# Twenty modulation tiles summed on VectorE during the projection stage of a two-layer trunk

## The reference

```python
mod = jnp.einsum('bd,lde->lbe', jax.nn.silu(c), mod_w) + mod_b[:, None, :]
for l in range(DEPTH):
    sh_m, sc_m, gt_m, sh_f, sc_f, gt_f = jnp.split(mod[l], 6, axis=-1)
    h = modulate(rms_norm(x, norm_w[l, 0]), sh_m, sc_m)
    y = hgrn2_ssd_mixer(...)  # layer 0: HGRN2 and SSD heads;  layer 1: rwkv7_mixer(...)
    x = x + gt_m[:, None, :] * y
    h = modulate(rms_norm(x, norm_w[l, 1]), sh_f, sc_f)
    x = x + gt_f[:, None, :] * grouped_moe(...)
```

## Time and profile before

| | us |
|---|---|
| time, median of 3 runs | 1276.27 (1276.25 to 1276.28) |
| the profiled execution's own time | 1273.94 |
| its span in the trace | 1272.2 |
| PE busy | 1162.0 (91%) |
| DVE busy | 398.7 (31%) |
| ACT busy | 268.5 (21%) |
| POOL busy | 84.7 (7%) |
| HBM read | 307.55 MB, 243 GB/s over the span |

### The profile page before, as it was taken

One profiled execution on the slowest core, in us unless ns is written; L12 is line 12 of the kernel. 1 busy time (PEld: TensorE's weight loads), 2 busy tenths in 40 slices (PEclk: granted clock), 3 DMA queues, 4 the chain that ended last, 5 costly groups with the idle time before them and its releaser, 6 DMA issues.

```text
span 1272.2 us, 15796 instructions
## 1 busy us (share of the span) xinstructions
PE 1162.0 (91%) x6545; PEld 742.2 (58%) x6546; DVE 398.7 (31%) x951; ACT 268.5 (21%) x443; POOL 84.7 (7%) x100
## 2 busy tenths in 40 slices
PE   4899999998898799999989699979988799989896
PEld 2775688873486544455444378648875544544353
DVE  0141322374611411111111584964432411111113
ACT  2212110414311211111101353233232111111113
POOL 5002121200000000000000001511000000000000
PEclk9899999999899799999999899989989899999898
DMA  9898462359884078929999830000378088999990
GB/s 353 274 387 318 166 223 108 132 194 381 350 294 169 1 259 308 394 108 394 394 394 367 285 133 1 1 1 2 132 268 328 1 319 305 395 394 394 394 372 33
DMA packets 139247, 309.35 MB, mean 243 GB/s; under 512 B 8032, under 2 KB 9404, under 8 KB 139196
## 3 DMA queue, kind: packets, MB, share of 16 engines
q1 hardware_dynamic: 138400, 307.39, 65.5%
q10 hardware_dynamic: 796, 1.23, 0.3%
HBM read 307.55 MB, written 1.05 MB: 243 GB/s over the span
## 4 chain that ended last, share of the span: by engine, by line
PE 66%; DMA 16%; DVE 8%; issue 4%; ACT 2%; SPq 2%; POOL 1%; ACTq 0%; DVEq 0%; POOLq 0%
DMA ring<-in_moe_w 14%; PE bank L1091 14%; PE bank L763 13%; PE bank L816 7%; PE bank L1115 4%; PE bank L1062 3%; PE bank L1055 3%; PE bank L796 3%; PE bank L774 2%; SPq L610 2%; DVE scratch L2347 1%; PE bank L879 1%; PE bank L1164 1%; DMA ring<-in_mod_w 1%; DVE arena L1896 1%
## 5 line engine op out<-in xcount | busy, mean ns | idle before, releaser
L1091 PE MATMUL bank<-ring,arena 128*64 128x512 f32 x992 | 230.8, 607 | 15.7 <-DMA ring<-in_moe_w 15.7
L763 PE MATMUL bank<-arena,ring 128*128 128x256 f32 x960 | 213.5, 384 | 2.7 <-ACT arena L1517 2.7
L763 PEld LDWEIGHTS bank<-arena,ring 128*128 128x128 f32 x960 | 183.6, 192 | 30.5 <-issue 5.3
L1091 PEld LDWEIGHTS bank<-ring,arena 128*64 128x64 f32 x992 | 76.0, 140 | 157.6 <-issue 147.6
L1115 PE MATMUL bank<-ring,arena 128*64 128x512 f32 x544 | 120.5, 595 | 0.0
L2221 DVE TENSOR_TENSOR arena<-arena,bank 128x512 f32<-128x512 f32 x17 | 11.7, 688 | 251.3 <-PE bank L1091 251.3
L816 PE MATMUL bank<-arena,ring 128*128 128x256 f32 x384 | 86.1, 388 | 2.9 <-issue 2.9
L816 PEld LDWEIGHTS bank<-arena,ring 128*128 128x128 f32 x384 | 74.8, 195 | 13.9 <-issue 3.2
L1062 PE MATMUL bank<-arena 128*128 128x256 f32 x336 | 79.0, 380 | 1.7 <-issue 1.7
L1115 PEld LDWEIGHTS bank<-ring,arena 128*64 128x64 f32 x544 | 37.6, 137 | 73.6 <-issue 73.6
L1055 PEld LDWEIGHTS bank<-arena 128*128 128x128 f32 x608 | 70.6, 195 | 13.8 <-issue 13.8
(11 more groups left out here) (362 smaller groups left out, 1269.9 us busy)
## 6 DMA issues: line engine op xcount, KB each, us to landing
ring<-in_moe_w SPq DMA_DIRECT2D x90, 2048.0 KB, 16.8
ring<-in_mod_w SPq DMA_DIRECT2D x24, 2048.0 KB, 11.8
ring<-in_ev_w_in SPq DMA_DIRECT2D x13, 2048.0 KB, 12.2
arena<-in_moe_w SPq DMA_DIRECT2D x6, 2048.0 KB, 16.8
ring<-in_od_w_rkv SPq DMA_DIRECT2D x6, 2048.0 KB, 12.3
ring<-in_ev_w_out SPq DMA_DIRECT2D x4, 2048.0 KB, 17.8
ring<-in_od_w_o SPq DMA_DIRECT2D x2, 2048.0 KB, 10.3
arena<-in_x ACTq DMA_DIRECT2D x1, 1024.0 KB, 9.0
```

The source lines that it names most:

```text
L763: mm = pe.matmul(ps[:, c * S:(c + 1) * S], w_cols(slot)[:, k, (2 * half + c) * P:(2 * half + c + 1) * P], src[:, k, :], start=(k == 0), st ...
L1091: mm = pe.matmul(bank[4 + half][e * C:(e + 1) * C, :], hgT[:, kb, e * C:(e + 1) * C], w_cols(slots[2 * half + e])[:, kb, :], start=(kb == ...
```

## The change

The modulation tiles 4 to 23 are no longer multiplied on PE. For each, `mod_sum(m)` on DVE forms the weighted sum of its eight blocks of 128 rows: one `tensor_scalar` and seven `scalar_tensor_tensor` over 128x512, each waiting for the one before. That leaves 128 partial sums for each column in one of four accumulators (`mod_acc`, in arena buffer 10). PE adds these over the partitions in `mod_direct(m)`: four matmuls with the accumulator as weights and one column of ones. The accumulators alternate, so `mod_sum(m)` waits until `mod_direct(m - 4)` is done (semaphore `mod_full`), and `mod_direct(m)` waits for `mod_summed`.

The tiles of layer 1 come into the projection stage: one modulation tile behind each of in-tiles 0 to 3, and two behind each of in-tiles 4 to 11. PE's `modulation_step` in the HGRN steps and heads is gone. DVE takes the results of both layers in one place, between the last score copies and the convolution. ACT waits for the last `mod_direct` before it writes `gT`, which lies in the same buffer as the accumulators. The four sums of weights 0 to 3 stay on PE.

```diff
     for n, j in enumerate((2, 3, 0, 1, 4, 5, 12, 10, 11, 8, 9, 6, 7)):
         first.append(("in", 0, j))
-        if MOD_FIRST + n < 12:
-            first.append(("mod", 0, MOD_FIRST + n))
-    first += [("mod", 1, j) for j in range(12)]
+        for _ in range(1 if n < 4 else 2):
+            if m < MOD_DVE:
+                first.append(("mod", m // 12, m % 12))
+                m += 1
...
+                if kind == "mod" and MOD_FIRST <= 12 * l_mod + j < MOD_DVE:
+                    sp.wait_ge(mod_summed, 12 * l_mod + j + 1 - MOD_FIRST)
...
+            def mod_direct(m):
+                pe.wait_ge(mod_summed, m - MOD_FIRST + 1)
+                for q in range(4):
+                    mm = pe.matmul(bank[6][:, 4 * m + q:4 * m + q + 1], mod_acc[m % 4][:, q * P:(q + 1) * P],
+                                   ones[:, 0:1], start=True, stop=True)
+                mm.then_inc(mod_full, 1)
...
-                if MOD_FIRST + n < 12:
-                    modulation(MOD_FIRST + n, bank[7])
-                elif MOD_FIRST + n == 12:
-                    mod_columns(1, bank[6])
+                for m in {4: (4, 5, 6), 5: (7, 8, 9), **{n: (2 * n - 2, 2 * n - 1) for n in range(6, 13)}}.get(n, ()):
+                    mod_direct(m)
...
+            act.wait_ge(mod_full, MOD_DVE)
             evac_T(gT, 0, ACT.Silu)
...
+            def mod_sum(m):
+                slot, count = mod_slot(m)
+                acc = mod_acc[m % 4]
+                dve.wait_ge(tile_landed[slot], 16 * count)
+                dve.wait_ge(mod_full, max(MOD_FIRST, m - 3))
+                link(ts_(acc, w_cols(slot)[:, 0, :], csilu[:, 0:1], None, ALU.mult))
+                for k in range(1, KB):
+                    ins = stt(acc, w_cols(slot)[:, k, :], csilu[:, k:k + 1], acc, ALU.mult, ALU.add)
+                    if k < KB - 1:
+                        link(ins)
+                ins.then_inc(mod_summed, 1)
...
+            mod_sum(MOD_FIRST)
             dve.wait_ge(proj_evac, 4)
...
             level_diff(0)
             level_diff(1)
+            for m in range(5, 10):
+                mod_sum(m)
...
             for i in range(8):
                 level_mult(i)
+                for m in range(10 + 2 * i, min(12 + 2 * i, MOD_DVE)):
+                    mod_sum(m)
                 if i < 7:
                     level_take(i)
...
-            dve.wait_ge(mod_cols, 2)
-            modulation(0, 4 * MOD_FIRST, 48, bank[6]).then_inc(mod_taken, 1)
+            dve.wait_ge(mod_full, MOD_DVE)
+            mod_take(0, 4 * MOD_FIRST, 48)
+            mod_take(1, 0, 48).then_inc(mod_taken, 1)
             dve.wait_ge(mod_taken, 2)
             gains(0, 1)
+            gains(1, 0)
+            gains(1, 1)
```

More of the change, by code:

```diff
@@ L59 @@
 MOD_FIRST = 4
+MOD_DVE = 24
 NSUB = 4
@@ L86, in weight_tiles @@
     first = [("mod", 0, j) for j in range(MOD_FIRST)]
+    m = MOD_FIRST
     for n, j in enumerate((2, 3, 0, 1, 4, 5, 12, 10, 11, 8, 9, 6, 7)):
         first.append(("in", 0, j))
-        if MOD_FIRST + n < 12:
-            first.append(("mod", 0, MOD_FIRST + n))
-    first += [("mod", 1, j) for j in range(12)]
+        for _ in range(1 if n < 4 else 2):
+            if m < MOD_DVE:
+                first.append(("mod", m // 12, m % 12))
+                m += 1
     first += [("out", 0, j) for j in range(4)]
@@ L237, in trunk @@
         mod_full = sem("mod_full")
+        mod_summed = sem("mod_summed")
         mod_row = sem("mod_row")
@@ L281, in trunk @@
         dtz = sem("dtz")
-        dtabs = sem("dtabs")
         dtln = sem("dtln")
@@ L339, in trunk, with mod_slot @@
         M = [dict(shared, **{n: sem(f"m{l}_{n}") for n in moe_names}) for l in range(LAYERS)]
-        mod_rows = [buf(10)[:, 0:W], buf(10)[:, W:2 * W], buf(1)[:, 0:W]]
-        slide = [buf(i)[:, 2 * W:2 * W + KB * 63].rearrange("p (k n) -> p k n", k=KB) for i in (10, 10, 1)]
-        MOD_GROUPS = ((0, MOD_FIRST), (MOD_FIRST, 12), (12, 24))
+        mod_rows = [buf(10)[:, 0:W]]
+        slide = [buf(10)[:, 2 * W:2 * W + KB * 63].rearrange("p (k n) -> p k n", k=KB)]
+        MOD_GROUPS = ((0, MOD_FIRST),)
         def mod_group(m):
             return [g for g, (a, b) in enumerate(MOD_GROUPS) if a <= m < b][0]
+        mod_acc = [buf(10)[:, i * W:(i + 1) * W] for i in (0, 1, 3, 2)]
+        def mod_slot(m):
+            return plan[0][places[0, "mod"][m]][1:]
         qT, kT, bT, zT, gT = blocks(2), blocks(4), blocks(5), blocks(11), blocks(10)
@@ L507, in wait_used @@
                 at = places[l, kind].index(n)
-                if kind == "mod":
+                if kind == "mod" and MOD_FIRST <= 12 * l_mod + j < MOD_DVE:
+                    sp.wait_ge(mod_summed, 12 * l_mod + j + 1 - MOD_FIRST)
+                elif kind == "mod":
                     sp.wait_ge(mod_full, 12 * l_mod + j + 1)
@@ L799, in modulation @@
                 mm.then_inc(mod_full, 1)
-            mod_next = [12]
-            def modulation_step():
-                if mod_next[0] < 24:
-                    if mod_next[0] == 12:
-                        pe.wait_ge(basics, 3)
-                    modulation(mod_next[0], bank[0])
-                    mod_next[0] += 1
+            def mod_direct(m):
[4 more added lines that the diff above has]
+                mm.then_inc(mod_full, 1)
             def out_projection(stage, first, n, srcs, ready):
@@ L929, in _ @@
                 mm.then_inc(o_full, 1)
-                modulation_step()
             pe.wait_ge(dt_ready, 1)
@@ L1006, in _ @@
             mm.then_inc(stat_full, 1)
-            pe.wait_ge(mod_taken, 3)
             out_projection(0, places[0, "out"][0], 4, lambda i: oa[:, i, :] if i < KB else yT[:, i - KB, :],
@@ L1595, in _ @@
             evac_xbc(0)
-            mod_evac(1, bank[7])
             level_exp(4)
@@ L1601, in _ @@
             act.wait_ge(dtz, 1)
-            act.activation(dts[:, 1, :], dts[:, 0, :], ACT.Abs).then_inc(dtabs, 1)
-            act.wait_ge(dtabs, 1)
+            link(act.activation(dts[:, 1, :], dts[:, 0, :], ACT.Abs))
             act.wait_ge(small_landed, 16 * 7)
@@ L1871, in modulation, with mod_take @@
                            by_chunk(cols("mod_b", 48 * l + a, 48 * l + b)), ALU.add)
+            def mod_sum(m):
[9 more added lines that the diff above has]
+                ins.then_inc(mod_summed, 1)
+            def mod_take(l, a, b):
+                c = 48 * l + a
+                return tt_(modT[:, l, a:b], bank[6][:, c:c + b - a], cols("mod_b", c, c + b - a), ALU.add)
             def gains(l, f):
@@ L2070, in _ @@
                     ssd_out((h - 4) // 2)
-            dve.wait_ge(mod_cols, 3)
-            modulation(1, 0, 48, bank[2]).then_inc(mod_taken, 1)
-            dve.wait_ge(mod_taken, 3)
-            gains(1, 0)
-            gains(1, 1)
             dve.wait_ge(stat_rstd, 5)
```

7 lines of the change are left out of this document (removed).

## The result

The changed kernel takes 1346.29 us (1345.57 to 1346.58, 4 runs) against 1276.26 us for the kernel before on the same chip (1275.72 to 1276.28, 4 runs), a ratio of 1.0517 (95% interval 1.0477 to 1.0558). The forecast was 1318 us, with a range of 1302 to 1330: slower was right, the size was not. The mean granted clock went from 0.957 to 0.907.

What follows compares the result with a forecast made beforehand. The prediction took PE to set the time, with other engines level at levels 0 and 6. Terms +5.4 +12.8 +5.1 +8.2 +4.3 +12.7 +2.5 -9.9 gave +41, so 1318 us on the median, range 1302 to 1330.

Steps and rivals of the forecast that it cites:

- the four waits: PE waits at levels 0 and 1 for DVE, level 6 for POOL's product, and the convolution for ACT's SiLU; 76%.
- The price of a sum: On DVE, one tile's `tensor_scalar` and seven `scalar_tensor_tensor` take 6.0 us, bounds 5.4 and 6.6.
- steps 1, 4 and 6: Added delay up to level 0, +5.4 us; from level 5 to level 6, +8.2; from level 7 to SiLU, +12.7.
- the term from SiLU to head 0: Between the convolution's SiLU and the SSD heads, PE restarts after a long idle spell: +2.5 us.
- rivals A and B: A: DVE has room, nothing waits, 1261 us, 3%. B: levels on time, only the convolution late, 1284 us, 7%.
- C: Rival: DVE becomes the bound at every level, with sums nearer 7.5 us or POOL's steps slower: 1335 us, 10%.
- D: Rival: transfers come late as SP waits for DVE ahead of each in-tile, some 5 us at two or three levels: 1330, 4%.
- Step 7: In the SSD heads, eight modulation steps at 1.53 us go, less two `ssd_out` of 0.9 that come later: -9.9 us.
- So I let it shift as a block: Everything behind the SSD heads (output projection, experts, layer 1) keeps its order and ring slots: no added time.
- Step 3: Levels 2 to 5: PE stays the bound, narrowly, with 2.6 us more modulation work and a 2.5 us restart: +5.1.
- Steps 2 and 5: Level 0 to level 1: DVE's late sum and a 2.5 us restart, +12.8. Level 6 to level 7: `mod_direct` and restart, +4.3.
- a changed length of these stages: Sign of being wrong: the stages behind the output projection change their length.

Runs made afterwards that it cites:

- first experiment: The changed kernel with 16 extra 128x512 matmuls, used by nobody, while PE waits for the convolution's SiLU: 1347.1 us, ratio 1.0495.

## Why the prediction was right and wrong

The direction, the four waits and their releasers were right, and the experiments on order bear them out one by one: 12.9 of the 20.6 us at level 1, all of the wait at level 6 and all 12.6 us at the convolution went by moving instructions that do the same work. The price of a sum (6.0 us), steps 1, 4 and 6 and the term from SiLU to head 0 hold within 0.6 us. Steps 4 and 6 hold term by term; at step 1 there was luck. VectorE was free for the takes 0.9 us sooner than forecast (125.1 for 126.0), and from there to level 0 it took 6.3 us for the 4.9 "as before", as the second half of the diagonal ran at a lower clock (3.52 us; all of it took 4.00 in before). The rivals A and B needed levels on time, and didn't come. C wanted TensorE to idle for VectorE at levels 2 to 5, but it was busy for 96.00 of 96.00 us there. D had transfers late: neither TensorE nor VectorE waited for one between level 0 and the convolution.

The forecast's terms add up to +41.1 us (its last line has 41.3, a slip of 0.2), the measure is +71.6. Of the 30.5 missing:

- **Step 7, the heads: 13.2 us.** "Eight at 1.53" took the pitch of heads 8 to 15 as a property of a head. It was one of a head at full clock. In the changed kernel the clock fell ahead of the third decay row, and from there on a head took 2.62. Where the clock was brought back (the block in head 3), the stretch took 53.2 us. From the forecast's own terms, 58.5 of before + 2.5 - 9.9, and 3.5 for the block, it would be 54.6: the mechanism was right, its clock was not. Removing the wide matmuls from the loop removed what had kept the clock up, or brought it back.
- **The last part: 7.4 us.** "So I let it shift as a block" was wrong by 0 to 10 us for any kernel of this set, as its clock differs from kernel to kernel. The prediction had named a changed length of these stages as a sign of being wrong.
- **Step 3, levels 2 to 5: 5.7 us.** Its restart behind level 1 cost 3.3 at the level (7.06 for 3.79) and 2.2 at the in-tile (16.21 for 14.03), 5.5 for the 2.5 forecast. The fall of the clock at level 3 with PE busy cost 1.9 + 1.5 us more; the column matmuls cost some 0.3 less, and durations that overlap a little make up the rest. This fall belongs to the change: in all ten traces of kernels with twenty sums level 3 took 5.5 to 6.3 us, and 3.8 in the four others. With twenty sums 1.8 us of one-column matmuls stand ahead of it, and in the others a wide step or half as many.
- **Steps 2 and 5: 3.6 us.** Restarts again: 5.0 us around level 0 (6.22 for 3.76, and 16.51 for 13.95 at in-tile 5) and 4.3 around level 6 (7.09 for 3.79, 15.07 for 14.03), for 2.5 each. I had read the price from two stretches behind 2.70 and 3.98 us idle. In the changed kernel, behind 6.52 to 11.41 us, it is about twice the 2.5. The length of the idle spell doesn't set it. At level 6 it was 4.8 us behind 3.21 us idle (first experiment: 7.09 for 3.79, 15.57 for 14.03), and behind 6.53 us it was 5.8 in the kernel with one block in head 3 (16.52 for 14.03) as against 4.3 behind 6.52 in the changed kernel.
- **Small terms: 0.6 us.** The squares ran slower (+0.9), and steps 1, 4, 6 and the term from SiLU to head 0 differ by 0.6 us at most and nearly cancel.

The Trainium skill, page "TensorE: Matmul & The Clock Gate", section "What's actually happening", says that the half rate is the default and that PE's recent activity lifts it. The restarts agree, and wide matmuls bringing the clock back do too. Its section "HAM oscillation — how this bites in real kernels" puts falls down to idle gaps. The fall in the 4.77 us ahead of the third decay row agrees with that. The others here don't: at level 3 the clock fell with PE busy throughout (208 to 216 us), from 368 to 400 us it stayed at 0.50 with PE busy throughout, and with the 4.77 us filled it fell all the same, so the measurement decides.

What stays open: why the clock fell in the loop with the wide work in heads 0 and 1 and not with it in heads 0 to 3 or in head 3; why it fell at level 3 in all ten traces with twenty sums, at level 5 in only four of them (5.5 to 6.3 us) and at level 2 in none, all of which follow the same matmuls; and why one block seems to have worked in two runs of four.

## What to carry to other kernels

Matmuls taken out of a loop of thin ones may have been what kept TensorE's clock up: price the loop at both levels, 1.5 and 2.6 us a head here, and look at the granted clock in windows in which PE is fully busy. A move of work to an engine with idle time pays only as far as it fits into the gaps between that engine's duties; twenty tiles cost 5%, eight gained 0.6%, so before giving up on a move try the part of it that fits. A wait behind moved work can be one of order: look for the one small instruction, here an addition of 0.5 us, that stands behind it.

## What the runs showed of the hardware

TensorE's granted clock stayed at 0.50 with the engine busy for 32.00 of 32.00 us, and fell at level 3 with it busy for 8.00 of 8.00 us. In the profiled run one block of eight matmuls of 128x512 brought it back to 1.00 within its 3.48 us, after which thin heads kept it for over 16 us. Behind idle spells of 3.21 to 11.41 us a restart cost 4.3 to 5.8 us in the cases above, whatever their length. The same last part of the program took from 923.2 to 933.0 us, with mean granted clocks from 0.953 down to 0.941. Seven linked sums of 128x512 took 5.48 us alone and 8.94 beside 4.65 us of GpSimd.
